# Modulation weights in blocks of 2048 rows, x loaded first, and opened products by pieces of two tiles

## The reference

```python
mod = silu(c) @ w_ada + b_ada                    # w_ada: 2048 x 6144
shift, scale, gate = split(mod, 3)               # 2048 each
h = rms_norm(x, g_pre) * (1.0 + scale) + shift   # 256 x 2048
proj = h @ w_in                                  # w_in: 2048 x 20032
q_mla, kv_a, z_mla, qkv_dil, z_dil, gl_mla, gl_dil = split(proj, ...)
```

## Time and profile before

| | us |
|---|---|
| three runs | 2391.74, 2392.48, 2392.79 (median 2392.48) |
| the profiled execution | 2392.98 |
| its span in the trace | 2391.7 |
| TensorE busy | 2358.8 |
| VectorE busy | 1472.7 |
| ScalarE busy | 1133.5 |

### The profile page before, as it was taken

One profiled execution on the slowest core, in us unless ns is written; L12 is line 12 of the kernel. 1 busy time (PEld: TensorE's weight loads), 2 busy tenths in 40 slices (PEclk: granted clock), 3 DMA queues, 4 the chain that ended last, 5 costly groups with the idle time before them and its releaser, 6 DMA issues.

```text
span 2391.7 us, 28776 instructions
## 1 busy us (share of the span) xinstructions
PE 2358.8 (99%) x11172; PEld 1957.4 (82%) x11172; DVE 1472.7 (62%) x2084; ACT 1133.5 (47%) x1478; POOL 87.3 (4%) x121
## 2 busy tenths in 40 slices
PE   8899999999999999999999999999999999999999
PEld 5577898988889898888888988888788788888777
DVE  6888675555455455776756675566765455455674
ACT  5333454544444554443444444554444545455453
POOL 0000000000000000000000100000100000000010
PEclk9999999999999999999999999999999999999999
DMA  9886643545554457887655655545665555555565
GB/s 385 314 319 249 186 143 128 178 154 192 186 179 128 143 175 245 289 290 257 216 190 182 193 165 170 162 158 189 227 208 192 167 177 175 176 163 178 188 217 179
DMA packets 135851, 478.99 MB, mean 200 GB/s; under 512 B 15794, under 2 KB 16050, under 8 KB 134690
## 3 DMA queue, kind: packets, MB, share of 16 engines
q1 hardware_dynamic: 130688, 458.42, 57.6%
q0 software_dynamic: 3728, 17.76, 2.0%
q10 hardware_dynamic: 1298, 0.97, 0.1%
HBM read 470.80 MB, written 6.29 MB: 199 GB/s over the span
## 4 chain that ended last, share of the span: by engine, by line
PE 92%; DVE 4%; ACT 2%; issue 1%; DMA 0%; SPq 0%; DVEq 0%; ACTq 0%
PE G L841 25%; PE G L843 25%; PE G L842 25%; PE A L852 4%; PE G L837 2%; DVE wlo L1466 2%; PE A L837 1%; PE A L841 1%; PE A L843 1%; PE A L842 1%; PE A L923 1%; PE A L903 1%; ACT whi L1124 1%; PE A L996 1%; DVE CP L1777 1%
## 5 line engine op out<-in xcount | busy, mean ns | idle before, releaser
L1466 DVE TENSOR_TENSOR wlo<-raw,whi 128x1024 fp32r<-128x1024 f32 (+3 forms) x772 | 912.6, 1186 | 692.5 <-ACT whi L1124 690.7
L1124 ACT ACTIVATE whi<-raw 128x1024 fp32r<-128x1024 f32 (+3 forms) x772 | 789.8, 1025 | 826.5 <-PE G L843 756.7
L841 PE MATMUL G<-whi,XH 128*128 128x512 f32 (+3 forms) x2800 | 1080.9, 386 | 8.7 <-DVE wlo L1466 6.0
L843 PE MATMUL G<-whi,XL 128*128 128x512 f32 (+3 forms) x2800 | 1065.1, 380 | 0.0
L842 PE MATMUL G<-wlo,XH 128*128 128x512 f32 (+3 forms) x2800 | 1064.1, 380 | 0.0
L841 PEld LDWEIGHTS G<-whi,XH 128*128 128x128 f32 x2800 | 525.9, 188 | 105.3 <-DVE wlo L1466 11.3
L843 PEld LDWEIGHTS G<-whi,XL 128*128 128x128 f32 x2800 | 525.5, 188 | 94.5
L842 PEld LDWEIGHTS G<-wlo,XH 128*128 128x128 f32 x2800 | 526.2, 188 | 90.3 <-issue 0.5
L1479 DVE CUSTOM_DVE_ANT_0 raw<-raw,dil 128x1024 f32<-128x1024 f32 x64 | 80.9, 1279 | 13.4 <-ACT dil L1107 7.4
L841 PE MATMUL A<-whi,XH 128*128 128x512 f32 x160 | 68.7, 429 | 7.4 <-DVE kept L1548 4.4
L1181 ACT ACTIVATE nat<-G 128x512 f32<-128x512 f32 (+3 forms) x98 | 54.1, 569 | 28.8 <-PE G L843 28.6
(11 more groups left out here) (230 smaller groups left out, 1600.9 us busy)
## 6 DMA issues: line engine op xcount, KB each, us to landing
raw<-in_weights SPq DMA_DIRECT2D x788, 512.0 KB, 4.1
raw<-in_weights SPq DMA_DIRECT2D x80, 384.0 KB, 3.1
raw<-in_weights SPq DMA_DIRECT2D x16, 288.0 KB, 3.0
spill<-nat POOLq DMA_DIRECT2D x8, 512.0 KB, 4.8
CP<-spill POOLq DMA_DIRECT2D x8, 512.0 KB, 6.7
raw<-in_weights SPq DMA_DIRECT2D x8, 336.0 KB, 3.2
FT<-in_xT SPq DMA_DIRECT2D x4, 512.0 KB, 7.4
kept<-in_weights SPq DMA_DIRECT2D x4, 512.0 KB, 12.7
```

Of the source, the lines that this page charges most:

```text
L841: pe.matmul(acc, xh[:, k, half], wh, start=(k == start), stop=False)
L843: ins = pe.matmul(acc, xl[:, k, half], wh, start=False, stop=(k == end - 1))
L1124: ac.activation(whi[r % NSPL][:, 0:2 * cols], raw[o.home[n]][:, 0:2 * cols], ACT.Copy).then_inc(hi_done, 1)
L1466: ve.tensor_tensor(wlo[r % NSPL][:, 0:2 * cols], raw[o.home[n]][:, 0:2 * cols], whi[r % NSPL][:, 0:2 * cols].bitcast(F32), ALU.subtract).t ...
```

## The change

- A modulation block has 2048 rows (1 MB), and one instruction reduces it. Such blocks have 4 buffers of their own (NADA), w_in's have 5, and MORE and halves are gone.
- x is loaded ahead of all weights. The 16 squared tiles are added down to one by VectorE (adds 1024, 1024, 1024, 512 and 256 wide), and one matmul with ones is left of 12.
- FT is multiplied by rst by itself (`normed`: tile 0, tile 1, tiles 2 and 3, then by fours in pieces "rst.n"); the scale column is made two tiles at a time (`scale_of`), and ScalarE applies scale and shift in one instruction (`tile_rows`).
- "open" is a piece of two tiles (seven in the walk instead of four in AFTER). It stands right behind the take of the block with the odd tile's shift.
- The first phase's slots stand in a table (`OPEN_SLOTS`), and products have three groups instead of four (`SEGMENTS`); spare holds three products' last group and is added when the product is finished.
- Whole slots: 0 to 3, then 5, 8, 11, 14, 17, and from 24 on every sixth instead of every fourth (16 in all, 20 before).
- The w_ada blocks stand behind slots 4 to 15 one each, then every third slot (`due`).
- ScalarE's squares and silus of c take turns.

```diff
-MORE = 6
+NADA = 4
-WHOLE = frozenset([*range(OPENING), *range(12, 22, 2), *range(24, 66, 4)])
-GROUPS = ((0, 2), (2, 4), (4, 8), (8, 12))
+OPEN_SLOTS = ((2, 0), (0, 0), (3, 0), (1, 0), (4, 0), (5, 0), (6, 0), (7, 0), (6, 2), (7, 2), (8, 0), (8, 2), (9, 0),
+              (9, 2), (GATE0, 0), (GATE0, 2),
+              (0, 2), (1, 2), (2, 2), (3, 2), (2, 4), (2, 6), (3, 4), (3, 6), (0, 4), (0, 6), (4, 2), (4, 4), (4, 6),
...
+SEGMENTS = {n: ((0, 2), (2, 8), (8, 12)) if n in (2, 3, 4, 5) else ((0, 4), (4, 8), (8, 12)) for n in PARTIAL}
+SPARED = (3, 4, 6)
+WHOLE = frozenset([*range(OPENING), 5, 8, 11, 14, 17, *range(24, 66, 6)])
@@ weight_plan
+        return [("ada", "w_ada", base + 128 * j, 1024, 0) for base in (2048, 0)]
...
+    plan += [scale[0], shift[0], slots[0], slots[1], scale[1], slots[2], shift[1], slots[3]]
+    later = [x for j in range(2, KT) for x in (scale[j], shift[j])]
+    due = [*range(4, 8), *range(8, 16), *range(17, 41, 3), *range(42, 66, 3)]
+    for n, slot in enumerate(slots[OPENING:], OPENING):
+        plan.append(slot)
+        plan += [x for x, at in zip(later, due) if at == n]
@@ AFTER
-    10: "open.1", 21: "open.2", 22: "late.0", 24: "rot.0", 28: "rot.1", 32: "rot.2", 34: "rot.3", 36: "rot.4",
-    42: "open.3", 64: "open.4", 66: "p1.0", ...
+    9: "rst.1", 13: "rst.2", 22: "late.0", 24: "rot.0", 30: "rst.3", 48: "rot.1", 50: "rot.2", 52: "rot.3", 54: "rot.4",
+    66: "p1.0", ...
@@ Order.items
+                if self.plan[n][0] == "ada" and self.plan[n][2] < 2048 and self.plan[n][2] // 128 % 2:
+                    self.walk.append(("piece", "open", self.plan[n][2] // 256))
@@ tensor_program
-            elif name[0] == "p" and name.endswith(f"_{STARTED[0]}") or s == OPENING or (name == "d0q0" and k >= 12):
-                pe.wait_ge(x_lo, k + 2)
+            else:
+                pe.wait_ge(x_lo, k // 2 + 1)
...
+        pe.matmul(P[3][:, 0:T], ones[:, :], sqx[:, 0, :], start=True, stop=True).then_inc(squares_summed, 1)
@@ scalar_program
+        def tile_rows(k):
+            ac.wait_ge(modulated, shift_no(k))
+            ac.activation(FT[:, k, :], FT[:, k, :], ACT.Identity, bias=mods[:, k:k + 1],
+                          scale=small[:, 40 + k:41 + k]).then_inc(h_ready, 1)
+        def pair_rows(j):
+            ac.wait_ge(h_ready, 2 * j + 2)
+            ac.activation(XH[:, 2 * j:2 * j + 2, :], FT[:, 2 * j:2 * j + 2, :], ACT.Copy).then_inc(x_hi, 1)
...
         squares(0)
+        silu_of_c(0)
+        squares(1)
+        silu_of_c(1)
+        squares(2)
+        squares(3)
+        silu_of_c(2)
         silu_of_c(3)
@@ vector_program
+                if f < 2:
+                    scale_of(f, 1, o.ordinal[n] - 1)
+                elif f < 16 and f % 2:
+                    scale_of(f - 1, 2, o.ordinal[n] - 1)
+                b = raw[o.home[n]][:, :]
+                ve.tensor_tensor_reduce(b, b, cs, 1.0, cols_[:, f:f + 1], ALU.mult, ALU.add,
+                                        mods[:, f:f + 1]).then_inc(modulated, 1)
...
+        def pair_rows(j):
+            ve.wait_ge(x_hi, j + 1)
+            ve.tensor_tensor(XL[:, 2 * j:2 * j + 2, :], FT[:, 2 * j:2 * j + 2, :],
+                             XH[:, 2 * j:2 * j + 2, :].bitcast(F32), ALU.subtract).then_inc(x_lo, 1)
...
+        take(0)
         ve.wait_ge(squares_summed, 1)
...
         ve.wait_ge(vector_step, t)
-        operand_rows(0, 1)
+        normed(0, 1)
+        take(1)
+        normed(1, 1)
+        normed(2, 2)
@@ sync_program
-        load(0)
-        load(1)
         for n in range(4):
             sp.dma_start(FT[:, 4 * n:4 * n + 4, :], i["xT"][:, 4 * n:4 * n + 4, :]).then_inc(x_landed[n], 16)
-        for n in range(2, len(plan)):
+        for n in range(len(plan)):
```

More of the change, by code:

```diff
@@ L106, in modulation @@
     def modulation(j):
[L107 to L120, removed]
+        return [("ada", "w_ada", base + 128 * j, 1024, 0) for base in (2048, 0)]
+    slots = [("w", "w_in", opened[n][1], 512, k) for n, k in OPEN_SLOTS]
+    scale, shift = zip(*(modulation(j) for j in range(KT)))
+    plan += [scale[0], shift[0], slots[0], slots[1], scale[1], slots[2], shift[1], slots[3]]
[4 more added lines that the diff above has]
+        plan += [x for x, at in zip(later, due) if at == n]
     for w, c0, cols, nkt in seq[:3]:
@@ L331, in product_runs @@
     first = [f"d0{x}{g}" for g in range(3) for x in "qkv"] + ["d0z", "m0z"]
[L332 to L338, removed]
+    for n, k in OPEN_SLOTS:
+        if n in RESIDENT:
+            part(first[n], k, k + 2)
+            continue
+        g = next(g for g, (lo, hi) in enumerate(SEGMENTS[n]) if lo <= k < hi)
+        run(f"p{g}_{n}", 512, "X", *SEGMENTS[n][g])
+        part(f"p{g}_{n}", k, k + 2)
     for n, name in enumerate(first):
@@ L436, in raw_homes @@
     def raw_homes(self):
-        plan, held, taken = self.plan, {}, 0
-        n_open = next(n for n in range(len(plan)) if plan[n][4] == 12 and plan[n][0] == "w")
+        held, taken = {}, {"w": 0, "ada": 0}
         self.home, self.before, self.nth = [], [], []
-        for n in range(len(plan)):
-            b = taken % (NRAW + MORE) if n < n_open else n % NRAW
+        for n, block in enumerate(self.plan):
             if n in self.blocks[:OPENING]:
-                b = NRAW + MORE + self.blocks.index(n)
-            else:
-                taken += 1
+                b = NRAW + NADA + self.blocks.index(n)
+            elif block[0] == "ada":
+                b = NRAW + taken["ada"] % NADA
+                taken["ada"] += 1
+            else:
+                b = taken["w"] % NRAW
+                taken["w"] += 1
             prev, count = held.get(b, (None, 0))
@@ L520, in counts @@
                 for name, times in signals(a, b).items():
-                    count[name] = count.get(name, 2 * (name in ("x_hi", "x_lo"))) + times
+                    count[name] = count.get(name, 1 * (name in ("x_hi", "x_lo"))) + times
                     self.after[(a, b, name)] = count[name]
@@ L718, in rope_views, with shift_no @@
         return x, ta, tb, c, s, dst.rearrange("p h (s r) -> p h s r", s=2)
+    def shift_no(k):
+        return next(o.ordinal[n] for n in range(len(plan)) if plan[n][0] == "ada"
+                    and plan[n][2] == 128 * (k if k < 2 else k | 1))
     def row_source(job):
@@ L759, in first_rows @@
                           start=True, stop=True).then_inc(side_full, 1)
-        def sum_of_squares(ks):
-            for k in ks:
-                ins = pe.matmul(P[3][:, 0:T], ones[:, :], sqx[:, k, :], start=(k == 0), stop=(k == 11))
-            return ins
         def open_products():
@@ L1232, in move_part @@
             g, n = int(name[1]), int(name[3:])
-            if g > 1 or (g == 1 and n not in spare):
+            if g == 1 or (g == 2 and n not in spare):
                 return
@@ L1536, in move_part @@
             for hf in range(2):
-                if g == 3 and n in spare:
-                    for x in (0, 1):
-                        bank, nth = use[f"p{x}_{n}"][hf]
-                        ve.wait_ge(moved[bank], nth)
-                    t = own(ve.tensor_tensor(e[:, hf, :], spare[n][:, hf, :], e[:, hf, :], ALU.add))
-                    ve.wait_ge(vector_step, t)
-                else:
-                    bank, nth = use[f"p{g - 1}_{n}" if n not in spare else f"p0_{n}"][hf]
-                    ve.wait_ge(moved[bank], nth)
+                bank, nth = use[f"p{g - 1}_{n}"][hf]
+                ve.wait_ge(moved[bank], nth)
                 product_done(name, hf)
```

123 lines of the change are left out of this document (55 added, 68 removed), and 2 rows, old and new, of the table AFTER.

## The result

The changed kernel takes 2395.01 us (median of 20 runs, 2394.04 to 2398.27); beside it the kernel before takes 2392.32 (20 runs, 2389.95 to 2395.03). The ratio is 1.0014, interval 1.0008 to 1.0019: 2.7 us slower. Forecast were 2391.0 and 1.5 us faster. The time lies in the range and under the 0.2% that one comparison of a few runs can tell, but with 20 runs the sign is plain, and it is the other one.

What follows compares the result with a forecast made beforehand. TensorE, busy 99%, was taken to bound the kernel. Opening -1.1, whole slots -2.8, stalls and clock +2.1 made -1.7 us: 2391.3 profiled, 2390.8 for the median, rounded 2391; range 2381 to 2397.

Steps and rivals of the forecast that it cites:

- Three more after slot 66 beside other work: Three products' adds put off past slot 66; dropped sums were to help VectorE only and give TensorE nothing.
- behind it nothing changes: After slot 66: TensorE's row carries the shift of -1.7 us unchanged to the end.
- Opening, -1.1: Start of the kernel: opened products begin at 21.0 instead of 22.06 us, 1.1 us earlier.
- rival 2: Opening later, by table-load drain (+1.4), x landing (+1.5), clock return (+1.5): 2395.5 at most, 2393 likely; chance 0.06.
- Its 22.4 for the opened products: Start of the opened products if the skill's table-load drain applied, 1.4 us later; the sum went without it.
- Slots 4 to 16: From slot 4's start S: VectorE and ScalarE queues stall slots 7, 12, 16; 10.5 us idle against 7.4, plus 1.8 clock.
- Transfers don't bound it: Up to slot 16, in-order queues decide, not DMA: slot 15's block lands at about 67 us, wanted at 75.
- Whole slots, -2.8: Slots 4 to 65: 50 split and 12 whole instead of 46 and 16, 177.7 us, 2.8 less.
- Rival 3: VectorE late at open pieces 4 to 7, first at slot 27: 2399 at 2 us each, 2395 at one; chance 0.12.
- The 16.06 kept for the opened products: Opened products to slot 4: the 16 matmuls again take 16.06 us, +-1.5 for when the clock comes back.
- The sum: Slot 66 at 227.0 instead of 228.76, -1.7 us: opening -1.1, whole slots -2.8, stalls and clock +2.1.

Runs made afterwards that it cites:

- experiment 1: Changed kernel without spare sums (third group added at once, none behind slot 66): 2392.13 us, ratio 1.0001 to the kernel before.
- experiment 4: Changed kernel with the first silu of c ahead of the first square, one table load less: 2393.59 us, ratio 1.0009 to the kernel before.
- Experiment 2: Changed kernel with each open piece put behind the next slot's takes: 2384.51 us, ratio 0.9968 to the kernel before.
- experiment 6: Changed kernel with every fourth slot whole again from slot 24 on: 2400.35 us, ratio 1.0036 to the kernel before.
- experiment 7: Kernel before the change, with every sixth instead of every fourth slot whole from slot 24 on: 2391.44 us, ratio 0.9999.
- experiment 5: Changed kernel with the first modulation block (1 MB) loaded ahead of x: 2398.86 us, ratio 1.0030 to the kernel before.
- experiment 8: Changed kernel with the constants' piece late.0 behind slot 17 instead of slot 21: 2395.73 us, ratio 1.0015 to the kernel before.
- experiment 3: Changed kernel with each open piece put behind the eviction that follows the slot: 2394.72 us, ratio 1.0006 to the kernel before.

## Why the prediction was wrong, point by point

- **"Three more after slot 66 beside other work" and "behind it nothing changes": wrong, and the largest step that failed.** The forecast gave these adds no cost. The waits read for it were those of the first phase; at 285 us VectorE was already last before, by 1.08 us, and no term had that place. They cost 2.0 us by 293 and 0.6 more by 307 in the profile, and 2.9 in the time (experiment 1).
- **Opening, -1.1: wrong.** Measured +0.45. The mean rate over 8 us gave x's first quarter at 3.5; it came at 5.07, and the adds ended 1.65 late, the 1.5 that rival 2 had for it. The rest held: 2.27 for the reduction exactly, the second table load 1.28 and on the path (experiment 4). The rule of the Trainium skill ("ScalarE: Activation LUTs", What ACT_TABLE_LOAD costs) of a drain of about 1.38 us beside the load is not borne out here: the load ends at 7.42 and the silu starts at 7.43, and without the load all is 1.40 earlier, not 2.66. Its 22.4 for the opened products lies near the measured 22.51 by chance: x's late landing made it.
- **Slots 4 to 16: right.** Slot 7's wait 1.87 for 2.4, slot 12 at S+28.8 for S+28.45, slot 16 at S+46.1 for S+46.1, its wait 4.29 for 4.6 and the low clock behind it. The total of the waits was 7.2 for 10.5, because the low clock behind slot 7, not forecast, ate most of slot 12's (in experiment 1, where the clock stayed up behind slot 7, slot 12 waits 2.12). In all six profiles with this order of pieces slot 16 starts at S+46.1, whether the clock fell behind slot 7 or not: the chain of VectorE and ScalarE sets it, as the forecast said.
- **Transfers don't bound it: right.** Experiment 2 moves slot 17 by 9 us on the same transfers.
- **Whole slots, -2.8: right in size** (wholes 17.05 apart from slot 30 to slot 60, the 17.1 that was computed; 3.2 between slot 24 and 66 in experiment 6). In the kernel before, 1.7 of it vanishes in waits for wlo (experiment 7).
- **Rival 3's place, slot 27, cost 0.93** where the forecast had nothing. Rival 3 had put it down to VectorE's chain being too long; it was a small transfer that ScalarE waited for. Its other three pieces cost nothing: from slot 27 to slot 66 TensorE has no wait.
- **The 16.06 kept for the opened products: within its +-1.5.** It came out as 15.02, a gain of 1.0 that no step of the change made.
- **The sum.** Forecast of the span 2390.0, measured 2393.1: opening +1.5, opened products -1.0, slots 4 to 66 +0.9 (slot 27), behind slot 66 +1.75. The last is counted from 228.76, as the forecast did.
- **The rest of +2.7.** The profiles differ by 1.4 in span, the medians by 2.7. Opened products to slot 4 took 15.02 in the profile after, and 14.8 to 16.2 in the ten other executions of that code, seven of them at 15.8 or above; in the kernel before it took 16.06, and 14.90 in experiment 7. So the profile after is one with a short opening; with equal ones the spans differ by 2.4. That this makes up the 1.3 us is argued from those spreads, not shown by a run that holds the clock fixed.

With the 1.04 put back, slot 66 stands at 229.4 instead of 228.41, against 229.26 before: the phase as a whole gained nothing, and what follows it lost 2.2.

## What to carry to other kernels

A piece in which two engines hand work to each other belongs behind the copies that the next matmuls need, not in front of them: that one change of order was worth 10.5 us here, seven times the forecast effect of the whole change. Work that is put off to a later phase must be priced at its new place, by the waits there, even where the phase under study is over. And a wait that is removed is worth only the distance to the next late operand in the same queue: follow the chain to the point where both versions meet again.

## What the runs showed of the hardware

The clock's fall after a short wait is no fixed thing. Slot 7 waits 1.87 or 1.88 us in six profiles: in the one after and in experiment 4 the matmuls behind it stand 0.43 apart for some 3 us, in experiments 1, 5, 6 and 8 they don't. Likewise 1.91 us idle at 285 lowered it in the profile after, and 1.92 at the same place in six experiments (2 to 6 and 8) didn't; 1.39 us at 59.14 in the kernel before didn't either. The wait of 1.79 us near 2232 stands in all thirteen profiles: behind it the clock stayed up in seven and fell in six, the kernel of experiment 7 among them, and that cost 1.3 to 2.9 us of span. A difference of that size between two single profiles says nothing until this place has been compared.

Its return varies as well. The second group of the opened products in the profile after, and then the start of the same code in experiment 8's, whose edit comes much later:

```profile
25.92 1.88 PE L781 MATMUL G<-kept,FT 128*128 128x512 f32 x4
```

```profile
22.57 3.78 PE L781 MATMUL A<-kept,FT 128*128 128x512 f32 x4 [7.05 <-ACT FT L1112]
26.14 2.73 PE L781 MATMUL G<-kept,FT 128*128 128x512 f32 x4
```

Both stand behind the same 7.05 us idle. The first group takes 3.57 us (22.51 above) and 3.78, the second 1.88, the full-clock length, and 2.73: with what follows a difference of 1.0 us up to slot 4 that no edit made.

A transfer of 8 KB on ScalarE's queue took 6.56 us to land (99.97 above) while the DMA moved 414 GB/s, and 6.1 to 6.9 in the nine other profiles that have it at that place. It took 3.5 us in the kernel before at the same piece, at 333 GB/s, 4.2 in experiment 7, at 325, and 4.3 in experiment 8, four slots earlier, at 356. That the load on the DMA sets this time is a reading of these rows; no run varies it alone.
